# Padded steps between the SBUF tiles that TensorE streams and loads, in a two-block fp32 kernel

## The reference

```python
h = rmsnorm(x, g) * (1.0 + scale_m) + shift_m           # first block
p_q, p_k, p_v, p_g, p_gk, p_cq, p_ckv, p_kr, p_ga, p_gb = split(h @ w_in)   # 2048 x 11344
y_gla = (gated linear attention(q, k, v, p_gk) gated by p_g) @ gla_wo
y_mla = (latent attention: (lat_q @ mla_wuq), (lat_kv @ mla_wukv)) @ mla_wo
x = x + gate_m * ((sigmoid(p_ga) * y_gla + sigmoid(p_gb) * y_mla) @ w_out)
g, u = split(h_f @ ffn_w_in); x = x + gate_f * ((silu(g) * u) @ ffn_w_down)
for l in range(2):                                      # second block, two layers
    proj = rms_norm(x) @ w_in_2[l]                      # 2048 x 6656
    mixed = concat(retention, differential attention, gated recurrence)
    x = x + rms_norm(mixed @ w_out_2[l], g)
```

## The kernel before

| tile | offset | step |
|---|---|---|
| `whi` | 20480 | 4096 per slot, 2048 per kk |
| `wlo` | 36864 | same |
| `h` (H2), high at +0, low at +1024 | 53248 | 2048 per k |
| `xs` | 86016 | |
| work area `wk2` | 114176 | |
| work area `wk` (`ogh`, `ah`, `lkh` and others) | 124416 | 1024 per k |

## Time and profile before

### The profile page before, as it was taken

One profiled execution on the slowest core, in us unless ns is written; L12 is line 12 of the kernel. 1 busy time (PEld: TensorE's weight loads), 2 busy tenths in 40 slices (PEclk: granted clock), 3 DMA queues, 4 the chain that ended last, 5 costly groups with the idle time before them and its releaser, 6 DMA issues.

```text
span 2656.0 us, 34047 instructions
## 1 busy us (share of the span) xinstructions
PE 2565.4 (97%) x12367; PEld 2157.0 (81%) x12367; DVE 1686.8 (64%) x2174; ACT 1276.3 (48%) x1812; POOL 76.9 (3%) x116
## 2 busy tenths in 40 slices
PE   3889999999999999999999999999999999999999
PEld 3888887888887887788888888889888987888887
DVE  6887776776766755567655545566656655566664
ACT  3345455444555444444433444455655545565553
POOL 0000000000000000000000000002000101100000
PEclk9999999999999999999999999999999999999999
DMA  9975665887676765687756666556465465555564
GB/s 364 344 253 157 185 205 175 301 301 266 206 249 197 231 212 169 213 278 258 250 190 195 192 190 186 184 188 192 146 190 169 141 213 145 173 178 175 148 201 135
DMA packets 280002, 554.18 MB, mean 209 GB/s; under 512 B 24463, under 2 KB 45693, under 8 KB 279197
## 3 DMA queue, kind: packets, MB, share of 16 engines
q1 hardware_dynamic: 274048, 541.79, 63.9%
q0 software_dynamic: 3168, 7.12, 0.8%
q10 hardware_dynamic: 2620, 3.09, 0.3%
HBM read 549.83 MB, written 2.10 MB: 208 GB/s over the span
## 4 chain that ended last, share of the span: by engine, by line
PE 88%; DVE 4%; ACT 4%; issue 2%; DMA 1%; SPq 0%; POOL 0%; DVEq 0%; ACTq 0%
PE gp L831 81%; PE tp L831 5%; PE tp L834 2%; ACT whi L1269 1%; DVE wlo L1877 1%; DMA raw_first<-in_ada_w_dram 1%; DVE acc L1883 1%; ACT L1269 0%; DVE xs L1877 0%; ACT hraw L1269 0%; SPq L814 0%; ACT sx L1269 0%; DVE stat L2201 0%; DVE sx L1877 0%; DMA raw<-in_mla_wuq_dram 0%
## 5 line engine op out<-in xcount | busy, mean ns | idle before, releaser
L1877 DVE TENSOR_TENSOR wlo<-raw,whi 128x1024 fp32r<-128x1024 f32 (+1 forms) x830 | 986.3, 1197 | 705.8 <-ACT whi L1269 702.5
L831 PE MATMUL gp<-whi,h 128*128 128x512 f32 (+1 forms) x4352 | 1372.8, 389 | 11.8 <-DVE h L1877 5.5
L1269 ACT ACTIVATE whi<-raw 128x1024 fp32r<-128x1024 f32 (+1 forms) x830 | 851.7, 1037 | 680.4 <-PE gp L831 552.1
L831 PEld LDWEIGHTS gp<-whi,h 128*128 128x128 f32 x4352 | 816.3, 188 | 170.4 <-issue 18.4
L831 PE MATMUL gp<-wlo,h 128*128 128x512 f32 (+1 forms) x2176 | 835.4, 384 | 0.0
L831 PEld LDWEIGHTS gp<-wlo,h 128*128 128x128 f32 x2176 | 410.4, 189 | 72.8 <-issue 1.7
L1883 DVE SCALAR_TENSOR_TENSOR acc<-raw,cact,acc 128x1024 f32<-128x1024 f32 x149 | 190.4, 1278 | 7.6 <-DMA raw<-in_ada_w_dram 6.8
L831 PE MATMUL gp<-whi,ah 128*128 128x512 f32 x352 | 138.0, 392 | 0.0
L831 PE MATMUL gp<-whi,al 128*128 128x512 f32 x352 | 137.1, 390 | 0.0
L831 PE MATMUL gp<-wlo,ah 128*128 128x512 f32 x352 | 137.0, 389 | 0.0
L831 PE MATMUL gp<-h,whi 128*128 128x256 f32 (+1 forms) x528 | 106.8, 299 | 20.6 <-ACT whi L1269 10.6
(11 more groups left out here) (331 smaller groups left out, 2606.1 us busy)
## 6 DMA issues: line engine op xcount, KB each, us to landing
raw<-in_w_in_dram SPq DMA_DIRECT2D x310, 512.0 KB, 4.4
raw<-in_ffn_w_in_dram SPq DMA_DIRECT2D x176, 512.0 KB, 4.5
raw<-in_ada_w_dram SPq DMA_DIRECT2D x158, 512.0 KB, 4.7
raw<-in_w_out_dram SPq DMA_DIRECT2D x96, 512.0 KB, 4.4
raw<-in_ffn_w_down_dram SPq DMA_DIRECT2D x88, 512.0 KB, 4.3
raw<-in_w_in_dram SPq DMA_DIRECT2D x64, 384.0 KB, 3.5
raw_first<-in_ada_w_dram SPq DMA_DIRECT2D x34, 512.0 KB, 8.5
raw<-in_gla_wo_dram SPq DMA_DIRECT2D x32, 512.0 KB, 5.5
```

Of the source, the lines that this page charges most:

```text
L831: return e.matmul(o, l, r, start=start, stop=stop)
L1269: return e.activation(o, i, f, **kw)
L1877: return e.tensor_tensor(o, a, b, op)
```

## The change

The weight tiles get 4 floats behind each row tile of 512: a step of 2064 bytes per kk and 4128 per slot. The tile `h` gets 16 floats behind each k: a step of 2112 bytes. The matmuls that stream both halves of `h` at once name them as one run of 512 floats. `stat` is cut from 832 to 448 floats so that all fits. The other activation tiles keep their steps of 1024 bytes and move with their area: `wlo` now begins at 36992, `h` at 53504, `xs` at 87296, `wk2` at 113920 and `wk` at 124160.

```diff
+W_PAD, H_PAD = 4, 16
@@
-    WHI = take("whi", [NW, 2, 512], F32R)
-    WLO = take("wlo", [NW, 2, 512], F32R)
+    WHI = take("whi", [NW, 2, 512 + W_PAD], F32R)[:, :, :, 0:512]
+    WLO = take("wlo", [NW, 2, 512 + W_PAD], F32R)[:, :, :, 0:512]
     h_off = used[0]
-    H2 = take("h2", [KD, 2, S], F32R)
-    HH, HL = H2[:, :, 0, :], H2[:, :, 1, :]
+    H2 = take("h2", [KD, 2 * S + H_PAD], F32R)
+    HH, HL = H2[:, :, 0:S], H2[:, :, S:2 * S]
@@
-    stat = take("stat", [832])
+    stat = take("stat", [448])
@@
-                        mm(o, h_, H2[:, k, :, :].rearrange("p a b -> p (a b)"), nth == 0, False)
+                        mm(o, h_, H2[:, k, 0:2 * S], nth == 0, False)
@@
-                        mm(o, wh[:, kk, fs], H2[:, k, :, :].rearrange("p a b -> p (a b)"), nth == 0, False)
+                        mm(o, wh[:, kk, fs], H2[:, k, 0:2 * S], nth == 0, False)
```

More of the change, by code:

```diff
@@ L690, in scol @@
             a = sum(m for _, m in scols.values())
-            assert a + n <= 832
+            assert a + n <= 448
             scols[name] = (a, n)
```

## The result

The changed kernel takes 2693.38 us (2693.15 to 2693.61), against 2656.16 us before: a ratio of 1.0139, with a 95% interval of 1.0122 to 1.0157. That is 37 us or 1.4% slower. The profiled execution took 2693.15 us with a span of 2691.3 us, at a granted TensorE clock of 0.994 of full (0.995 before).

What follows compares the result with a forecast made beforehand. TensorE bounds the kernel, by matmul count times start-to-start interval. Wide products 28.6 us plus narrow ones 2 make 30.6 us; 91% of it, 28 us, on 2656 gives 2684 us, 1.05% slower; range 2640 to 2715 us.

Steps and rivals of the forecast that it cites:

- Steps 1 and 2: Weight-tile conversions writing two runs (52 and 38 ns more at most, taken as 0); moved base addresses and shortened `stat`: 0.
- Step 3: 512-column matmuls on TensorE: new tile distances keep intervals from settling, 4 ns on each of 7,158, 28.6 us.
- the broken stretch behind transposes: Ten TensorE intervals after four transposes, 231.0 ns each against 226.7 settled: 4.3 ns, upper bound of the price per interval.
- The lower bound of 1.9 ns: From job `gk`, loading 80 weight columns: 348.6 ns per pair of matmuls against 346.7 settled; lower end of the price.
- The narrow products: TensorE's 384- and 256-column products: less than 3 us together in either direction, taken as 2 us more.
- The factor 0.91: Share of TensorE's time with `gp` products that the chain holds, 91%; left 28 us of 30.6 us on the path.
- No effect: Rival: TensorE's interval swing comes from the moments of loads and streams, not addresses; 2656 us, give or take 4; chance 0.22.
- A shorter settled rhythm: Rival: some distance holds TensorE's intervals 2 ns or a bit more under today's; 16 us less, 2640 us; chance 0.15.
- The fixed part vanishes: Rival: other distances spare the 13.3 ns each TensorE product pays beyond its columns; up to 87 us less, 2569 us; chance 0.05.
- The long interval becomes the rule: Rival: each weight load meets the stream badly on TensorE, +9 ns per interval; 59 us more, 2715 us; chance 0.08.

Runs made afterwards that it cites:

- the shifted kernels: No pads, all tiles behind the weights moved by 64, 256 or 192 bytes against the kernel before: 2703.62, 2656.81 and 2668.47 us.
- the streams: Kernels computing nothing of the reference: lists of 72 or 54 matmuls at chosen tile offsets; 512-column float32r takes 226.7 ns at distance 0, 233.3 at 64.
- the five slower kernels: Against the kernel before: both pads 2693.38 us, only weights padded 2694.78, only `h` padded 2679.29, tiles behind the weights moved by 64 bytes 2703.62, by 192 bytes 2668.47.

## Why the prediction was right, and where it wasn't

**The sum against TensorE's interval.** The time lies in the range, and the signs came: the FFN run took 174.93 us (174.4 forecast), the output runs 86.05 (85.8), and the rows by shape are 4 or 5 ns longer (4). (The 389 ns quoted there from the earlier trace rows is the median of the earlier trace rows; the earlier trace rows has means of 390 to 396.) The reading that the kernel is a count of matmuls times an interval held. The difference of 37.2 us is the difference of the intervals, and the unbroken pieces of the chain of the shifted kernels have the streams' intervals: 233.3, 226.7 and 228.9 ns at 64, 256 and 192.

**Steps 1 and 2, no cost for two-run conversions and moved bases.** Right. The conversions stay at 1058 and 1223 ns, and the kernel shifted by 256 bytes with the short `stat` takes the time of before. The upper bounds of 52 and 38 ns were each far from the truth, because they put all the intercept of a duration down to the second run.

**Step 3, direction.** Right: the new distances cost. But the border isn't 512 bytes, since odd multiples of 256 are as good.

**Step 3, mechanism.** Half right. "The rhythm changes from matmul to matmul and doesn't settle" describes what is seen in the padded kernel, but it is only one part of the cause: in the streams changing adds 1.3 to 2.5 ns, and the values passed through cost 1.9 to 3.6. A constant distance of 64 bytes settles at once and costs 6.6 ns, more than the changing ones. The last sentence of the prediction, that a mean over the distances might be the wrong tool, was the right question: a mean over a table of constant distances, which I didn't have, falls short of the changing streams by 1.3 to 2.5 ns.

**Step 3, price.** 4 ns per settled interval was forecast. The intervals of 512 columns now have a mean of 231.65, 5.0 above 226.67. That 4 came so near was in good part luck: the broken stretch behind transposes (4.3 ns) is at distance 0, so it shows the settling alone and nothing of what a distance costs, which the prediction didn't count. The lower bound of 1.9 ns came from `gk`, whose 80 loaded columns have a price of their own. Neither row measured what a distance costs with 128 columns loaded. A stream of 72 matmuls at one distance would have, and nothing in the trace of before could.

**The narrow products.** I took +2 us; they came to +1.2 us for 384 columns and -1.1 us for 256, so nothing.

**The factor 0.91.** It assumed that the 9% of TensorE's time with large products which the chain doesn't hold is hidden. Summed over intervals, the five slower kernels should differ from the one before by 37, 33, 22, 52 and 12 us, and measured 37, 39, 23, 47 and 12. Together that is 158 against 156, or 153 with the 34 us of the execution with only the weights padded that had the higher clock: the factor would be about 1. But the kernel shifted by 64 alone gives 0.9, and so do the spans of the profiled executions, from which the intervals come: without the one at the lower clock they differ from the one before by 114 us where the sums have 123. So the factor lies between 0.9 and 1, and the runs don't fix it. A possible reason for 1, argued and not tested: the other engines wait for TensorE before their part of the chain begins, so that part starts later by as much as the matmuls ahead of it. With 5.0 x 7,158 = 35.8 us and no factor, the sum would have been within 2 us of the result. The 9 us that it lacked are 7 from the price and 3 from the factor, with 2 back from the narrow products, and 1 from intervals that weren't settled before either.

**The rivals.** *No effect*: fell. What the Trainium skill says of two independent read ports (TensorE: Matmul & The Clock Gate, Part 2, step 1) doesn't agree with float32r here, where moving either tile alone by 16 or 64 bytes changes the interval; by what mechanism, no run shows. For bf16 and plain float32 the streams agree with it. *A shorter settled rhythm*: none of the 17 distances within 256 bytes that were tried does it for 512 columns, though for 256 columns the steady value at 64 is 2.2 ns shorter. *The fixed part vanishes*: 10.9 of the 13.3 ns belong to float32r, as the bf16 streams show, and no distance removes them; why float32r has them is open. *The long interval becomes the rule*: something near it exists, at 6.6 ns and not 9 for most distances; with one of these throughout, the kernel takes 2703.62 us. It wasn't this change, which meets cheaper distances as well.

## What to carry to other kernels

Where a kernel is bound by float32r matmuls that stream 512 or 384 columns and load 128, keep the distance between the streamed and the loaded tile a multiple of 256 bytes and both on multiples of 64. A pad between the two cost up to 7.5 ns in 227 at each matmul, both tiles 4 bytes off a multiple of 64 cost 11, and nothing in the wait times of the profile says so. (At 256 streamed columns distance 0 is among the slowest, by 2 to 3 ns.) Read it from an unbroken piece of the chain divided by its count. If a cost isn't in the trace, the nearest row can be confounded, as the row with 80 loaded columns was: look for what else differs in it before it becomes a bound.

## What the runs showed of the hardware

- The interval of 512-column float32r matmuls with 128 loaded columns depends on the distance between loaded and streamed tile. With the streamed one on a multiple of 512 it is, modulo 256 bytes, 226.7 ns at 0 and 240, 228.8 at 192, 232.4 at 128, 233.3 at most others, 234.2 at 96. It isn't smooth, and no rule for it was found.
- Where the distance changes between such values from matmul to matmul, 1.3 to 2.5 ns are added to their mean; where it changes by 256 or 512 bytes, nothing.
- It also depends on where both lie within 64 bytes: at equal offsets of 4, 8 and 16 bytes 237.7, 231.1 and 230.0 ns; at 32, 64 and 128 bytes 226.7. With the streamed tile alone at 16 it is 231.7, where the same distance with the streamed tile at 0 gives 226.7.
- For 256 columns distance 0 is among the slowest (120.0 ns), 96 and 240 give 117.4; in the kernel shifted by 192 bytes it was 115.3.
- With 80 loaded columns 512 streamed ones take 233.3 ns at distance 0 and 226.7 at 192; with 32 loaded, 230.7 to 231.7 at all three distances tried. With 128 loaded, 128 streamed ones take 111.7 ns.
- bf16 (215.8 ns for 512 columns, 109.2 for 256) and plain float32 (215.8 per pass of 256 columns) show none of this.
